# Four weight roundings moved to other places in ScalarE's order around an attention loop

## The reference

```
proj = h @ w_in[i]
q, k, v, z, xbc, dt_raw, g_logit = jnp.split(proj, IN_SPLITS, axis=-1)
ya = _window_attention(q, k, v, sinks[i]) @ w_out_attn[i]
ys = _ssd(xbc, z, dt_raw, ...) @ w_out_ssd[i]
gates = jax.nn.sigmoid(g_logit.reshape(b, s, 2, d) + b_gate[i])
mix = (gates[:, :, 0, :] * ya + gates[:, :, 1, :] * ys) @ w_out[i]
```

## Time and profile before

| what | value |
|---|---|
| time, median of 3 runs | 947.07 us (946.57 to 948.12) |
| profiled execution, its span | 947.1 us |
| TensorE busy (matmul) | 840.8 us, 89% of the span |
| VectorE busy | 426.3 us, 45% |
| ScalarE busy | 176.5 us, 19% |
| GpSimd busy | 151.3 us, 16% |
| TensorE's share of the chain that ended last | 83% |

### The profile page before, as it was taken

How to read it: one execution, slowest core, us unless ns; L and a number is a source line. 1 busy time by engine, 2 the same in 40 slices (tenths; PEclk the granted TensorE clock), 3 DMA queues, 4 the chain that set the end, 5 groups by cost and what they waited for, 6 DMA issues and landing times.

```text
span 947.1 us, 11294 instructions
## 1 busy us (share of the span) xinstructions
PE 840.8 (89%) x4489; PEld 584.5 (62%) x4489; DVE 426.3 (45%) x780; ACT 176.5 (19%) x331; POOL 151.3 (16%) x74
## 2 busy tenths in 40 slices
PE   0599997799999999999999998999999999999910
PEld 0488787788888885444448887756565556555600
DVE  6999534455688883112365763112111211121128
ACT  4222223453232220000002010111111111111112
POOL 6734741110123111000004000000000000000032
PEclk9999998899999999999999999999999999999965
DMA  9524231111121226230007462359999999999452
GB/s 307 193 90 89 82 97 45 45 45 46 46 78 56 57 78 233 78 126 31 21 0 253 148 206 106 97 201 359 357 357 371 361 360 356 367 363 358 153 183 106
DMA packets 119296, 163.42 MB, mean 173 GB/s; under 512 B 14412, under 2 KB 102614, under 8 KB 118742
## 3 DMA queue, kind: packets, MB, share of 16 engines
q1 hardware_dynamic: 113184, 139.68, 45.1%
q0 software_dynamic: 3072, 12.63, 3.7%
q10 hardware_dynamic: 2998, 10.53, 2.8%
HBM read 148.15 MB, written 14.68 MB: 172 GB/s over the span
## 4 chain that ended last, share of the span: by engine, by line
PE 83%; DVE 8%; DMA 4%; ACT 2%; issue 2%; POOL 0%; ACTq 0%; SPq 0%; DVEq 0%; POOLq 0%
PE psum L732 23%; PE psum L1010 14%; PE psum L1022 12%; PE psum L1037 6%; PE psum L941 6%; PE psum L931 6%; PE psum L980 4%; PE psum L922 3%; DMA ring<-in_w_in_dram 2%; DVE arena L1378 2%; ACT arena L1090 2%; DVE arena L1377 2%; PE psum L871 2%; PE psum L891 1%; PE psum L982 1%
## 5 line engine op out<-in xcount | busy, mean ns | idle before, releaser
L732 PE MATMUL psum<-ring_r 128*128 128x512 f32 (+1 forms) x768 | 213.2, 363 | 2.6 <-DVE arena L1549 1.3
L732 PEld LDWEIGHTS psum<-ring_r 128*128 128x128 f32 x768 | 139.4, 194 | 26.1 <-issue 2.4
L1010 PEld LDWEIGHTS psum<-arena 128*128 128x128 f32 x1088 | 125.5, 194 | 28.4 <-issue 25.1
L1010 PE MATMUL psum<-arena 128*128 128x128 f32 x1088 | 131.6, 280 | 2.9 <-DVE arena L1702 2.9
L667 POOL TENSOR_TENSOR ring_r<-ring,ring_r 128x2048 fp32r<-128x2048 f32 x20 | 93.4, 4670 | 205.3 <-ACT ring_r L1090 205.3
L1090 ACT COPY arena<-psum 128x512 f32<-128x512 f32 (+3 forms) x104 | 58.5, 582 | 351.8 <-PE psum L948 139.8
L1022 PE MATMUL psum<-ring,arena 128*64 128x512 f32 x512 | 113.4, 595 | 7.9 <-ACT arena L1090 7.9
L732 PE MATMUL psum<-arena_r,ring_r 128*128 128x512 f32 x256 | 100.4, 392 | 0.0
L1797 DVE SCALAR_TENSOR_TENSOR arena<-arena,psum 128x256 f32<-128x256 f32 x16 | 6.7, 421 | 186.5 <-ACT arena L1268 186.5
L1022 PEld LDWEIGHTS psum<-ring,arena 128*64 128x64 f32 x512 | 37.1, 137 | 73.9 <-issue 65.5
L695 POOL DMA_INDIRECT ring<-y_rows,rowsU x8 | 8.1, 1017 | 389.4 <-ACT arena L1090 387.2
(11 more groups left out here) (240 smaller groups left out, 875.8 us busy)
## 6 DMA issues: line engine op xcount, KB each, us to landing
ring<-in_w_exp_gate_dram SPq DMA_DIRECT2D x32, 1024.0 KB, 12.1
ring<-in_w_exp_up_dram SPq DMA_DIRECT2D x32, 1024.0 KB, 12.5
ring<-in_w_exp_down_dram SPq DMA_DIRECT2D x32, 1024.0 KB, 9.1
ring<-in_w_in_dram SPq DMA_DIRECT2D x18, 1024.0 KB, 5.3
y_rows<-arena ACTq DMA_DIRECT2D x16, 512.0 KB, 7.6
y_rows<-arena POOLq DMA_DIRECT2D x4, 1024.0 KB, 7.3
ring<-in_w_out_ssd_dram SPq DMA_DIRECT2D x4, 1024.0 KB, 7.4
ring<-in_w_out_dram SPq DMA_DIRECT2D x4, 1024.0 KB, 11.0
```

The source lines that it names most:

```text
L732: t = mm(o, a, b, start=(first and j == 0), stop=(last and j == 2))
L1010: t = mm(o[:, k, :], h[:, i, c:c + P], onehot[:, buf, i, :], start=(i == 0), stop=(i == NT - 1))
```

## The change

The four calls `part(10)` to `part(13)` of ScalarE get new places: `part(10)` stands behind `probs_out(0)`, `part(11)` behind `probs_out(2)`, `part(12)` behind `probs_out(4)` and `part(13)` behind `probs_out(6)`. Nothing else is edited. The casts themselves, their order among each other, the loads, GpSimd's subtractions and all other operations stay as they are.

```
             for j in range(4):
                 act.wait_ge(s_pe_q, j + 1)
                 copy(qT[:, j, :], bank(("q", j))).then_inc(s_q_read, 1)
-                if j % 2:
-                    part(10 + j // 2)
                 if j == 1:
...
                 A(z_part(n), bank(("z", n)).rearrange("p (i n) -> p i n", i=2), ACT.Tanh, scale=0.5)\
                     .then_inc(s_tz_done, 1)
-                if n in (1, 3):
-                    part(12 + n // 2)
...
                 if n:
                     attn_out(n - 1)
                 probs_out(n)
+                if n % 2 == 0:
+                    part(10 + n // 2)
             attn_out(7)
```

## The result

The changed kernel takes 950.89 us (947.58 to 953.45, 12 runs), the kernel before beside it 947.83 us (946.57 to 948.93, 12 runs): a ratio of 1.0033, with a 95% interval of 1.0022 to 1.0044. It is slower, by 3.1 us. The forecast was 945.0 us, within 934.8 to 947.8. The profiled span is 949.0 us, where it was 947.1 us.

What follows compares the result with a forecast made beforehand. TensorE's attention loop was bound by exponentials queued behind ScalarE casts awaiting weight slices. After port conflicts 4.8 us of gain remained, less 2.7 for the clock: 2.1 us off 947.1, so 945.0 us, range 934.8 to 947.8.

Steps and rivals of the forecast that it cites:

- The places and the port: Attention loop: landing waits vanish at the new cast places, but GpSimd's subtractions block VectorE; 4.8 us left at full clock.
- L1488's loss of the 0.11 us: Steps 3, 5, 7: GpSimd starts 0.11 us before VectorE's negation and blocks it; TensorE idles 3.25, 3.25, 4.3 us.
- Rival (a): Steps 3, 5, 7: VectorE's negation starts first and only L1497 waits; gain 11.7 us, 935.4 us; chance 20%.
- I charge 2.7 in all: Loop: total price in us for TensorE's half clock after the three new idle times, each between 0 and 2.4.
- the nearest row: Ahead of 590.48 us: idle time of 2.87 us, then 64 matmuls took 9.05 us, not 7.36; a clock price of 1.7.
- part of the slow time passes in ScalarE's copy: Behind step 7: a reason given for charging less than 1.7 us for each of the three idle times.
- rival (d): Steps 3, 5, 7: half clock costs 2.4 us after each idle time, 2.4 us slower, 949.5 us; chance 5%.
- What stands at 228 us stands at the end: After the loop: TensorE is the chain and loads follow its progress, so the loop's 2.1 us gain carries through unchanged.
- the waits for landings: Loop: TensorE idles 6.08, 4.66 and 1.39 us because casts awaiting weight slices hold up ScalarE's exponentials; the move removes this.
- Rival (c): Loop: no collision to speak of between GpSimd's subtractions and VectorE; gain 16.6 us, 930.5 us; chance 2%.
- the row at 517: At 517 us: a VectorE operation started 0.11 us after GpSimd's took 0.97 us; evidence that the negation loses.

Runs made afterwards that it cites:

- negation-first run: Changed kernel with two small VectorE operations swapped, so the negation releasing the exponentials comes ahead of sink less maximum: 941.29 us, ratio 0.9926.
- GpSimd after the negation: Changed kernel with each of GpSimd's four moved subtractions also waiting for VectorE's negation of the step behind it: 941.88 us, ratio 0.9926.
- second fill run: Changed kernel with TensorE repeating attend(2) and attend(4) four times and attend(6) five times, same result: 944.84 us, ratio 0.9968.
- gate casts alone: Kernel before with only part(12) and part(13) moved, behind probs_out(4) and probs_out(6); the two z casts stay ahead of the loop: 953.69 us, ratio 1.0068.

## Why the prediction was wrong

**The places and the port: right.** The gain up to the end of step 2 was 12.7 us by the forecast; the copy behind its transposes starts 25.45 us after scores(0) (162.29 less 136.84), where it started 38.11 us after it (175.55 less 137.44): 12.7. The start of step 1 is 0.70 us late, where 0.8 was forecast. L1488's loss of the 0.11 us, the point at which I chose, holds in all three steps, with 3.21, 3.21 and 4.27 us of idle time for 3.25, 3.25 and 4.3. At full clock the loop would have gained 91.30 - 86.61 = 4.7 us; the forecast had 4.8. Rival (a), VectorE first, is what the negation-first run and the run with GpSimd after the negation make by force; its 935.4 lacks the clock too.

**The clock: the step that failed.** The term is "I charge 2.7 in all", from a bound of 0 to 2.4 us each. The second fill run measured 5.7 us in this loop, and the windows share them out as 1.57, 1.53 and 2.59. For the loop the sign of the result hung on this one term: 4.8 - 2.7 is a gain, 4.8 - 5.7 a loss of 0.9, where 1.0 was measured. Two errors are in it. 2.7 is 0.9 for each, where the nearest row gave 1.7 and every idle time of over 2.8 us in the rows had lowered the clock. And I priced the last one low, since "part of the slow time passes in ScalarE's copy"; it was the dearest, 2.59 us here and 3.45 in the run with the gate casts alone, both over the 2.4 that I held for the upper end. The range is also narrower than its own words: its top of 947.8 is a price of 5.5 us, while three times the bound of 2.4 us is 7.2 and gives the 949.5 of rival (d). That the copy's 1.10 us, idle time of TensorE as well, prolong the slow stretch is my reading of it and was not tried alone.

**"What stands at 228 us stands at the end": wrong by 1.7 us.** The later stage dips to half its clock in eight of the thirteen profiles, and never in the two of the kernel before. With the loop's 1.0 us it makes 2.7 of the 3.1 us measured; the rest is less than what executions of one kernel differ by. Its cause stays open. The moment at which the stage begins, counted from scores(0), repeats within 0.1 us in the two kernels that have several profiles, and so does the length of the stage. But the moments have no plain order: no dip at 360.6 (two kernels), 366.5 and 377.2 us, a dip at 369.0, 369.4, 372.8, 375.2, 378.2 to 378.3 and 382.1. What does divide the thirteen profiles is step 7: where GpSimd's subtraction held up an operation of VectorE there, the dip is there too (eight), and where it did not, there is none (five). This holds even where the added matmuls left 0.31 us of idle time in step 7. How that would reach 285 us further on no run shows, and none changes one of the two alone.

**The other steps.** That the waits for landings would go was right. Rival (d), the clock eats more than is won, was the case; I gave it 5%. Its point of decision was 2.2 us for each idle time; the loop's clock cost 1.9 on the mean, a loss of 1.0 us that alone would have been no measurable change, and the later stage's 1.7 us took it past 0.2%. Rival (c), with 16.6 us of gain where nothing collides, was called possible only with a shorter subtraction; two other placements reached it to 0.04 us (91.30 - 74.66 = 16.64) with a subtraction of the same length put some 4 us later. The free stretch of VectorE that it fits into was to be read in the trace of before, and I had not looked for it.

## What to carry to other kernels

A move out of one engine's queue moves the work that follows on other engines too: here the cast was free at its new place, and the subtraction behind it met the one small operation that everything waits for. So list, for one steady step, at which times VectorE runs operations with two operands in SBUF or of the kind of this negation, and put GpSimd's block in the gap between them; 0.1 us of order was worth some 10 us here. And where a change trades one idle time of TensorE for another, charge each of 2 us or more with the 1.5 to 3.5 us of half clock that they cost here; that term can be larger than the one the change is about.

## What the runs showed of the hardware

An operation of VectorE on 128x4 elements, of 0.17 us, takes 4.49 us when it starts 0.11 us after GpSimd's subtraction of 128x2048, and 0.17 us when it starts 0.09 us before it. The Trainium skill says so on the page "SBUF — State Buffer", section "Who interferes with whom": who issues first has the shared ports for the whole instruction. These runs agree, for a tensor_scalar and a tensor_tensor alike. Two rows of the kernel before do not agree with "the whole": L1664 starts 0.11 us behind GpSimd's TENSOR_SCALAR of 2.77 us and takes only 0.97 us, and the TENSOR_TENSOR behind it, L1668, takes its usual time under the same operation. So the row at 517 that the prediction leaned on shows that the later one waits, but not for how long.

```profile
518.11 0.17 DVE L1668 TENSOR_TENSOR arena<-arena 128x16 f32<-128x16 f32 x1
```

TensorE's clock falls to half after idle times shorter than I had taken: 2.22 us were enough, 1.63 us were not (the third idle time in the second profile of before, where the eight transposes behind it take 1.09 us):

```profile
194.30 1.09 PE L808 MATMUL psum<-arena 128*128 128x128 f32 x8 [1.63 <-DVE arena L1499]
```

The price of the same idle time of 3.21 us was 1.5 us in one kernel and 2.7 in another, yet it repeats within 0.1 us in the three profiles of the changed kernel. And work that nobody needs, 10 repeats of 0.99 us, made the changed kernel 6 us faster, 5.7 of them in the loop, by keeping the clock up.
